# A fifth tile for the rows of the last two experts, scattered behind four tiles that are normalized earlier

## The reference, cut to what matters

```python
def expert_rows(args):
    xb, e = args
    h = jax.nn.silu(xb @ w_e_gate[e]) * (xb @ w_e_up[e])
    return h @ w_e_down[e]
...
y = jax.ops.segment_sum(y_rows * row_w[:, None], row_tok, num_segments=N + 1)[:N]
...
moe = _hier_moe(x, w_group, b_group, w_exp_router, b_exp_router, w_e_gate, w_e_up, w_e_down)
return _layer_norm(DEEPNORM_ALPHA * x + moe, ln2_g, ln2_b)
```

## Time and profile before

| | us |
|---|---|
| median of 3 runs | 1254.37 |
| lowest and highest | 1253.46, 1254.44 |
| the profiled execution | 1253.62 |
| its span, first to last instruction | 1251.6 |
| TensorE busy | 1226.5 |
| DVE busy | 674.8 |
| ACT busy | 427.9 |

### The profile page before, as it was taken

The page is one execution under the profiler, slowest core; times in us unless marked ns, Lnnn a source line. Parts: engine busy times, 40 slices in busy tenths (PEclk is TensorE's granted clock), DMA queues, the critical chain, the costliest instruction groups (busy, mean ns, idle before and its releaser), DMA issues.

```text
span 1251.6 us, 16410 instructions
## 1 busy us (share of the span) xinstructions
PE 1226.5 (98%) x6166; PEld 824.6 (66%) x6166; DVE 674.8 (54%) x1066; ACT 427.9 (34%) x619; POOL 60.6 (5%) x67
## 2 busy tenths in 40 slices
PE   9999999999999999999999999999999999999887
PEld 8888888888888888888888886333343334333333
DVE  6497765336365347338334757454555455544447
ACT  6778773223342333333243422311111111111115
POOL 0000000000000000000005200100000000000000
PEclk9999999999999999999999999999999999999998
DMA  7333323363323223222223599999999999999995
GB/s 244 103 98 91 102 64 89 107 169 91 93 68 101 84 67 101 84 84 84 84 68 101 171 395 421 393 412 410 417 413 414 409 414 416 416 407 415 411 424 210
DMA packets 144574, 286.10 MB, mean 229 GB/s; under 512 B 11909, under 2 KB 109301, under 8 KB 120960
## 3 DMA queue, kind: packets, MB, share of 16 engines
q1 hardware_dynamic: 141200, 278.85, 59.9%
q0 software_dynamic: 2544, 4.25, 1.0%
q10 hardware_dynamic: 768, 2.16, 0.4%
HBM read 284.91 MB, written 4.33 MB: 231 GB/s over the span
## 4 chain that ended last, share of the span: by engine, by line
PE 86%; DMA 9%; DVE 3%; ACT 1%; issue 1%; SPq 0%; DVEq 0%; ACTq 0%; POOL 0%; POOLq 0%
PE bank L1582 18%; PE bank L1584 18%; PE bank L1583 18%; PE bank L1925 15%; DMA m_raw<-in_w_e_up_dram 9%; PE bank L1957 7%; PE bank L1981 4%; PE bank L1909 1%; DVE wo_lo L929 1%; PE bank L1667 1%; PE bank L1950 1%; PE bank L1737 1%; PE bank L1658 0%; PE bank L1660 0%; PE bank L1659 0%
## 5 line engine op out<-in xcount | busy, mean ns | idle before, releaser
L929 DVE TENSOR_TENSOR w_lo<-raw,w_hi 128x1024 fp32r<-128x1024 f32 x120 | 148.3, 1239 | 181.5 <-ACT w_hi L586 180.3
L1925 PE MATMUL bank<-m_raw,xe 128*64 128x512 f32 x984 | 233.3, 598 | 10.5 <-DMA m_raw<-in_w_e_up_dram 8.9
L1582 PE MATMUL bank<-xt_hi,w_hi 128*128 128x512 f32 (+1 forms) x584 | 226.7, 388 | 0.3 <-DVE xt_lo L929 0.3
L1584 PE MATMUL bank<-xt_hi,w_lo 128*128 128x512 f32 (+1 forms) x584 | 225.6, 386 | 0.0
L1583 PE MATMUL bank<-xt_lo,w_hi 128*128 128x512 f32 (+1 forms) x584 | 225.5, 386 | 0.0
L925 DVE TENSOR_TENSOR x<-x,bank 128x1024 f32<-128x1024 f32 x120 | 141.1, 1218 | 99.5 <-PE bank L1981 98.5
L586 ACT ACTIVATE w_hi<-raw 128x1024 fp32r<-128x1024 f32 x120 | 126.3, 1058 | 160.4 <-PE bank L1584 157.8
L1925 PEld LDWEIGHTS bank<-m_raw,xe 128*64 128x64 f32 x984 | 70.6, 136 | 132.3 <-issue 130.7
L1582 PEld LDWEIGHTS bank<-xt_hi,w_hi 128*128 128x128 f32 x584 | 109.7, 188 | 23.5 <-issue 1.9
L1584 PEld LDWEIGHTS bank<-xt_hi,w_lo 128*128 128x128 f32 x584 | 109.7, 188 | 22.4
L1583 PEld LDWEIGHTS bank<-xt_lo,w_hi 128*128 128x128 f32 x584 | 109.7, 188 | 21.7
(11 more groups left out here) (286 smaller groups left out, 1674.9 us busy)
## 6 DMA issues: line engine op xcount, KB each, us to landing
m_raw<-in_w_e_gate_dram SPq DMA_DIRECT2D x64, 1024.0 KB, 26.1
m_raw<-in_w_e_down_dram SPq DMA_DIRECT2D x61, 1024.0 KB, 26.3
m_raw<-in_w_e_up_dram SPq DMA_DIRECT2D x59, 1024.0 KB, 25.5
raw<-in_w_in_dram SPq DMA_DIRECT2D x88, 512.0 KB, 3.8
raw<-in_w_ret_o_dram SPq DMA_DIRECT2D x16, 512.0 KB, 3.4
raw<-in_w_lru_o_dram SPq DMA_DIRECT2D x16, 384.0 KB, 3.4
m_split<-in_w_e_up_dram SPq DMA_DIRECT2D x10, 512.0 KB
raw<-in_w_out_dram SPq DMA_DIRECT2D x8, 512.0 KB, 3.8
```

The lines of the kernel that those rows point to most:

```text
L929: return dve.tensor_tensor(dst, a, b_r.bitcast(F32), ALU.subtract)
L1582: pe.matmul(dst, sh, mh, start=first and x == 0, stop=False)
L1584: ins = pe.matmul(dst, sl, mh, start=False, stop=last and x == n - 1)
L1925: last = pe.matmul(bank[side:side + ROWS, 0, :], xe[:, 4 * half + k, :], weights(w, FE * k, FE), start=half == 0 and k == 0, stop=half == ...
```

## The change

The rows of experts 30 and 31 are kept in a fifth tile. Its partitions 0 to 63 are the list of expert 30, and 64 to 127 that of expert 31. `late_rows` starts at zero in pass 24, and from pass 25 on TensorE makes one more sum a pass, `late_sums`: the rows of expert e-1 laid on the fifth tile's rows by `late_pick` (four matmuls into bank 2:4), which DVE adds (`add_late`). ACT takes the two experts' own input rows times alpha from `xg` (`base`), and DVE adds them in pass 30. The four other tiles get no part of experts 30 and 31: they are complete when expert 29 is added, and are normalized in pass 30 and behind it, between the work on expert 31. Rows in them that belong to the fifth tile come out wrong at first; POOL overwrites them last by an indirect transfer of `late_out` to the output, which waits for the four stores.

The constants it needs (the token numbers as a row, and ln2's two rows spread over all partitions) are made by TensorE in passes 23 to 27 from 16 KB loaded in pass 4, instead of by the two broadcasts at the end. To make room the ring has 20 slots from unit 152 on. DVE scales all five tiles. Some semaphores are merged.

```diff
+SHRINK, FEWER = 152, 20
+SHARED = (GROUPS - 1) * PER_GROUP
+CONSTS = SHARED - 1
...
-                    sp.wait_ge(m_done, n + 1 - MRING)
+                    sp.wait_ge(m_done, n + 1 - (MRING if n < SHRINK else FEWER))
...
+            pool.wait_ge(stored, 16 * TT)
+            pool.wait_ge(f_late, 2 * TT + 2)
+            pool.indirect_dma_start(out[0], bass.IndirectOffsetOnAxis(ap=late_idx[:, 0:1], axis=0), late_out[:, :], None,
+                                    bounds_check=last_x, oob_is_err=False).then_inc(scattered, 16)
...
+                if e > SHARED:
+                    pe.wait_ge(z_added, 4 * (e - 1) + 3)
+                    pe.wait_ge(late_pick_ok, e - SHARED)
+                    late_sums(bank[:, 2:4, :], late_pick, y_hi, y_lo, True).then_inc(late_made, 1)
                 if e + 2 < EXPERTS:
+                    if CONSTS < e <= CONSTS + 5:
+                        pe.wait_ge(consts_out, e - CONSTS)
                     turn_x(e + 2)
...
+                if CONSTS <= e < CONSTS + 5:
+                    pe.wait_ge(xe_ok, e + 3)
+                    make_constant(e - CONSTS)
...
+            tile_moments(0)
             gate_rows(gu_unit(LAST), LAST)
+            act.wait_ge(eps_set, 1)
+            row_std(0)
             ht_out(LAST, ht_last)
-            rows_high(2)
+            tile_moments(1)
+            row_std(1)
             y_high(down_unit(LAST - 1), 1, y_hi, first_w[:, LAST - 1:LAST])
-            rows_high(3)
+            tile_moments(2)
+            row_std(2)
             y_high(down_unit(LAST), 4, y_hi_last, first_w[:, LAST:LAST + 1])
+            tile_moments(3)
+            row_std(3)
+            act.wait_ge(late_made, LAST - SHARED)
+            row_mean(TT, z_late, TT + 1)
...
+            def add_late(e):
+
+                n = e - SHARED
+                dve.wait_ge(late_made, n + 1)
+                dve.wait_ge(late_added, n)
+                z = late_rows[:, :].rearrange("p (b n) -> p b n", b=2)
+                tt(z, z, bank[:, 2:4, :], ALU.add).then_inc(late_added, 1)
```

More of the change, by code:

```diff
@@ L51 @@
 NEAR = 4
-SPARE = 2
+SPARE = 6
 def by_rows(ap):
@@ new lines, in moment_cols, with row_mean, row_squares @@
+            def moment_cols(t):
+                first = 12 * t + 1 if t < TT else 6
+                return (stats[:, first + x:first + x + 1] for x in range(3))
+            def row_mean(t, z, count):
+                mean, _, _ = moment_cols(t)
+                act.activation(unused[:, :].rearrange("q (c n) -> q c n", c=2), z, ACT.Identity, scale=-1.0 / D, accum_out=mean).then_inc(f_mean, 1)
+                act.wait_ge(f_mean, count)
+            def row_squares(t, count):
+                mean, squares, _ = moment_cols(t)
+                act.activation(unused[:, :], unused[:, :], ACT.Square, bias=mean, scale=-float(D), accum_out=squares).then_inc(f_squares, 1)
+                act.wait_ge(f_squares, count)
@@ L1544, in _ @@
                 dve.wait_ge(lists_in, 64)
-                for t in range(TT):
-                    dve.wait_ge(z_made, 4 * (LAST - 1) + t + 1)
-                    dve.tensor_copy(x2[:, t, :].rearrange("p (b n) -> p b n", b=2), z_end[t]).then_inc(z_added, 1)
+                build_pick(pick, first_t[:, LAST - 1:LAST])
+                build_pick(pick_last, first_t[:, LAST:LAST + 1])
+                add_z(4 * (LAST - 1))
                 with dve.Fori(0, MAX_OVERFLOW) as j:
@@ L1989, in combine_next, with late_sums, make_constant @@
                 pe.wait_ge(pick_ok, e + 1)
+                if e > SHARED:
+                    pe.wait_ge(late_added, e - SHARED)
                 combine(4 * e, tiles, [(pick, y_hi, y_lo)], e == 0)
+            def late_sums(pair, choose, high, low, first):
+                for y in (high, low):
+                    for b in range(2):
+                        side = ROWS * b
+                        last = pe.matmul(pair[:, b, :], choose[side:side + ROWS, :], y[side:side + ROWS, :], start=first and y is high, stop=y is low)
+                return last
+            def make_constant(k):
+                if k:
+                    pe.wait_ge(ln2_in, 32)
+                    row = ROWS + k - 1
+                    last = pe.matmul(bank[:, 4, :], ident[ROWS:ROWS + 4, row:row + 1].to_broadcast([4, P]), ln2_rows[ROWS:ROWS + 4, :], start=True, stop=True)
+                else:
+                    last = pe.matmul(bank[:, 4, 0:P], late_t[:, :].to_broadcast([P, P]), ident[:, :], start=True, stop=True)
+                last.then_inc(consts_made, 1)
             for half in range(2):
@@ L2050, in _ @@
             with pe.If(n_over > 0):
+                pe.wait_ge(pick_ok, LAST + 1)
+                pe.wait_ge(late_added, LAST - 1 - SHARED)
+                pe.wait_ge(f_late, 2 * TT + 2)
+                combine(4 * (LAST - 1), range(TT), [(pick, y_hi, y_lo), (pick_last, y_hi_last, y_lo_last)])
                 pe.wait_ge(z_added, 4 * LAST)
```

287 lines of the change are left out of this document (168 added, 119 removed).

## The result

The changed kernel takes **1263.76 us** in the median of 4 runs (1262.67 to 1266.18), the kernel before 1254.40 beside it. The ratio is 1.0078, with a 95% interval from 1.006 to 1.0095. More executions later gave 1265.18 us (5 runs). I had forecast 1257.9 us, with a range up to 1261.5: slower was right, the size was not.

What follows compares the result with a forecast made beforehand. The weight stream bounds the last loop passes, with TensorE 0.6 to 2 us to spare; then DVE bounds the tail. Loop +5.2, tail -3.9, last transfer +2.2 make +3.5 us on 1254.37: 1257.9 us, range 1252.0 to 1261.5.

Steps and rivals of the forecast that it cites:

- That it would be slower: Whole kernel: 1257.9 us forecast, 0.28% slower; chance of slower 0.60, within 0.2% 0.27, faster 0.13.
- The late sums: Last passes of the experts' loop: TensorE waits for DVE's tile 2 addition, 2.3 us more a pass, 1.8 of it waiting.
- The covered case: Rival in the loop: tile 2's addition comes before TensorE asks, G stays, 1252.7 us; chance 0.13.
- The constants' price: Three of the loop's last passes: each matmul spreading ln2's rows costs 0.5 us, 3 x 0.5 in all.
- The dearer end: Upper bound for constants in the loop: a matmul sharing nothing costs twice 0.5 us; G then 6.7 us later.
- Nothing else in the loop: Loop up to G: only the longer passes and constants cost time, +5.2 us; ring, tiny copies and merged semaphores nothing.
- G: End of expert 31's second gate/up half, 1224.99 in the old profile; forecast 5.2 us later, about 1230.2.
- The tail's term: From G to DVE's end: 3.9 us less than 24.17, DVE done at +20.25 with 2.84 us a tile.
- The end: Last transfer: POOL's scatter lands 4.2 us after issue instead of the plain store's 2.0; +2.2 us, bounds 0 to +6.1.
- the fit in the Trainium skill: Last transfer: 2.0 us fixed plus bytes at 436 GB/s, 2.6 us for the scatter; sum 1.6 us lower.
- My sign for failure of this step: End of the kernel: forecast is wrong if DVE's end and the span's end lie less than 3 us apart.
- The ring and the rest: Loop: 20 slots instead of 22 cost nothing (5 us once without cover); tiny copies, self-waits and merged semaphores nothing.

Runs made afterwards that it cites:

- e1: Changed kernel with the late sums and their wait moved behind the transposes and the first half of the down products; 1255.24 us, ratio 1.0009.
- e17: e16 without the four matmuls that spread ln2's rows (ACT writes zeros instead); 1259.13 us, 3.4 us less than e16.
- e16: Changed kernel with six useless matmuls ahead of the wait for tile 2's addition in passes 25 to 30; 1262.51 us; its profile is "the third column".
- e11: e6 with six useless matmuls put ahead of the added wait; 1257.48 us, ratio 1.0024.
- e6: Kernel before with only TensorE's wait for DVE's addition of tile 2 added from pass 25 on; 1264.61 us, ratio 1.0071.

## Why the prediction was right or wrong

That it would be slower was right. Four steps of the sum failed: the price of a constant, the lower clock (put at nothing), DVE's price for a tile that lies in SBUF, and the end.

**The late sums were right in mechanism and size.** They wait for DVE's addition, not for weights; 16.2 us a pass was forecast and 16.20 and 16.17 were measured. From the start of the last pair of the combine to the transposes it is 2.53 us instead of 0.23 (1203.55 to 1206.08, and 1211.12 to 1211.35 before), so 2.3 more, as forecast. Moving them off the wait gave the loop's whole loss back (e1). The covered case, to which I gave 0.13, did not occur: in this order DVE's addition comes too late. In e1, where the sums stand 2.5 us further on, they are covered, and still it takes 1255.24 and not the 1252.7 us of that case, because the tail's and the end's misses below remain.

**The constants' price was mis-sized**: 0.5 us for each, 1.05 measured (passes of 17.2 beside 16.2, and 3.4 us for the three in e17). My row, 16 in 3.65 us, counts instructions, two for each matmul; I read it as matmuls. So it is not eight pairs side by side at 0.45 us but four at 0.9. The dearer end that I named was the true one. This is 1.6 us of the miss.

**"Nothing else in the loop" was wrong.** I priced standing still as lost time only. The granted clock fell to half for 3.41 us behind some of these waits. In the changed kernel this is about 1.4 us of the median (0 to 3), in the profiled execution two stretches: 1.7 us before G and 1.1 in the tail (23.46 against 22.32).

**The tail's term failed in one step**: I took 2.84 us a tile from tiles read in PSUM for tiles that are now read in SBUF, where they take 3.59. Tiles 1, 2 and 3 lie on the path, 2.2 us together, and 22.32 less 20.25 is 2.1 (in e16 they are done 0.7, 1.4 and 2.1 us later behind G than forecast). The rest of that chain, with DVE as the bound and ACT's copy of ht_last ahead of tile 1, held.

**The end**: +2.2 forecast, +3.3 measured. The landing took 3.2 us, between my 4.2 and the 2.6 us of the fit in the Trainium skill, page "DMA: Bandwidth & Descriptors", section "Anatomy of one DMA — SWDGE (gpsimd) path". But I compared landings only, and that is the step that failed. Behind DVE's end POOL needs 0.86 us to start the transfer, and behind the landing 1.7 us pass, where the plain end had 2.41 for everything. My sign for failure of this step (under 3 us from DVE's end to the span's) did not occur.

**The ring and the rest** cost little, if anything: with the late sums moved, the five passes take 77.29 us against 77.32 with 20 slots and all the constants in them. The start of these passes lay 0.9 to 1.8 us later in the two profiles; it varies too where nothing ahead of it differs from the kernel before (1148.28 and 1148.73 in e11 and e6, beside 1147.67). Over all profiles it lies at 1148.2 us in the mean in these three and between 1148.2 and 1151.1, in the mean 1149.4, in the fourteen of programs with the fifth tile. So a cost of about a microsecond ahead of these passes, which I had put at nothing, is likely; no run isolates it.

Sum for the median, from the third column: +3.5 forecast; passes +1.5, tail +2.1, end +1.1, start +0.9 make +9.1 for that profile, and it is 1262.51 - 1254.23 = +8.3 for the medians (the profiled execution before lies 0.75 us under its median). The changed kernel itself is at +9.4; the lower clock is in that difference, which is no larger than what the runs leave open.

## What to carry to other kernels

A wait that is shorter than the slack of a stage wasn't free on TensorE: 1.6 us of standing still in a pass of 16 cost up to 1.7 us more in lower clock. Independent work in the gap, useless matmuls or the pass's own, removed it in all nine profiles that had it. Before work is moved from PSUM to SBUF, or to an idle engine, look at its strides and at who shares the memory: the same operation took 0.75, 1.1 or 1.6 us by these alone. And when one transfer replaces another at the end, price it from the last computing instruction to the end of the span, not from issue to landing: here the landings were equal and the ends 2.0 us apart.

## What the runs showed of the hardware

- Before the tail, the granted clock went to 0.50 in stretches of 3.41 us, each beginning 0.1 to 1.9 us behind the end of a wait of about 1.6 us, in passes in which TensorE worked for all but that wait. Six matmuls of 128 columns in the gap, twelve instructions and 1.60 us, kept it at 1.00 there.
- Strided float32 access in SBUF: DVE 1.1 us instead of 0.75 for 128 x 512, read or write; ACT 2.05 instead of 1.04 for 128 x 1024, read. A strided read of PSUM cost neither anything.
- POOL's addition of 128 x 512 took 1.65 to 2.04 us beside DVE, and made DVE's operation of 0.75 us up to 1.78 us long.
- A scatter of 0.27 MB from POOL, in an empty machine: 0.86 us to its start, 3.2 to landing, 1.7 until the end of the span; 2.0 us dearer in all than a plain store of 512 KB from SP, which also landed in 3.2.
